# Moving fillers and small steps in the RWKV/attention stage of a fused decoder layer

## What is computed

```python
def layer_forward(x, c, attn_cache, rw_prev, rw_wkv, t5_table, lw):
    mod = (jax.nn.silu(c) @ lw['w_mod'] + lw['b_mod'])[:, None, :]
    sh1, sc1, gt1, sh2, sc2, gt2 = jnp.split(mod, 6, axis=-1)
    h = rms_norm(x, lw['norm1'], NORM_EPS) * (1.0 + sc1) + sh1
    q, k, v, p_rw, g_a, g_b = jnp.split(h @ lw['w_in'], IN_SPLITS, axis=-1)
    ...
    o_a = swa(q, k, v, ...)          # window of 128 keys, 8 query heads, 2 KV heads
    o_b, new_wkv = rwkv7_mix(p_rw, ...)
    m = jax.nn.sigmoid(g_a) * (o_a @ lw['w_pa']) + jax.nn.sigmoid(g_b) * (o_b @ lw['w_pb'])
    x = x + gt1 * (m @ lw['w_o'])
    h2 = rms_norm(x, lw['norm2'], NORM_EPS) * (1.0 + sc2) + sh2
    return x + gt2 * moe_ffn(h2, *lw['moe']), ...

def rwkv7_step(S, inp):              # one token; the kernel does the prompt in chunks of 64
    r_t, w_t, k_t, v_t, kk_t, a_t = inp
    sa = jnp.einsum('bhvk,bhk->bhv', S, -kk_t)
    S = (S * w_t[:, :, None, :] + sa[..., None] * (kk_t * a_t)[:, :, None, :]
         + v_t[..., None] * k_t[:, :, None, :])
    return S, jnp.einsum('bhvk,bhk->bhv', S, r_t)
```

## Time and profile before

| | |
|---|---|
| median of 3 runs | 1316.26 us (1314.79 to 1317.28) |
| the profiled execution, its own time | 1316.26 us |
| its span in the trace | 1314.5 us (1.8 us lie around it) |
| mean granted clock of PE | 0.99 |
| PE busy | 1254.3 us (95%) |
| DVE busy | 452.8 us (34%) |
| ACT busy | 300.0 us (23%) |
| POOL busy | 52.3 us (4%) |
| moved by DMA | 467 MB, 355 GB/s over the span |

### The profile page before, as it was taken

The page is one execution under the profiler, slowest core; times in us unless marked ns, Lnnn a source line. Parts: engine busy times, 40 slices in busy tenths (PEclk is TensorE's granted clock), DMA queues, the critical chain, the costliest instruction groups (busy, mean ns, idle before and its releaser), DMA issues.

```text
span 1314.5 us, 21012 instructions
## 1 busy us (share of the span) xinstructions
PE 1254.3 (95%) x8339; PEld 621.5 (47%) x8339; DVE 452.8 (34%) x1035; ACT 300.0 (23%) x554; POOL 52.3 (4%) x66
## 2 busy tenths in 40 slices
PE   6999997999989999999999999999999999999997
PEld 5887776987733333333333333333333333333333
DVE  2055648436342332222332222332222223322225
ACT  3013441210122222212221211221211122212112
POOL 0000621200000000000000000000000000000000
PEclk9999999999979999999999999999999999999999
DMA  9976251148459999999999999999999999999993
GB/s 365 358 255 248 100 164 67 36 179 342 193 202 406 426 428 428 428 430 429 426 430 429 428 428 429 428 428 430 426 428 430 429 427 429 429 428 428 430 428 164
DMA packets 55606, 467.05 MB, mean 355 GB/s; under 512 B 5141, under 2 KB 7449, under 8 KB 29690
## 3 DMA queue, kind: packets, MB, share of 16 engines
q1 hardware_dynamic: 53354, 461.07, 84.4%
q0 software_dynamic: 1664, 5.20, 1.4%
q10 hardware_dynamic: 544, 0.13, 0.0%
HBM read 463.91 MB, written 5.09 MB: 357 GB/s over the span
## 4 chain that ended last, share of the span: by engine, by line
PE 72%; DMA 20%; DVE 5%; ACT 2%; issue 1%; SPq 0%; DVEq 0%
PE ps L1346 25%; DMA ring<-in_w 18%; PE ps L1373 13%; PE ps L1294 6%; PE ps L865 5%; PE ps L1319 4%; PE ps L855 2%; DMA ring<-in_w_in 2%; PE ps L1253 2%; PE ps L1354 2%; PE ps L1221 1%; PE ps L1301 1%; PE ps L834 1%; ACT PT L751 1%; PE ps L874 1%
## 5 line engine op out<-in xcount | busy, mean ns | idle before, releaser
L1346 PE MATMUL ps<-ring,PT 128*64 128x512 f32 x1536 | 338.9, 595 | 8.0 <-DMA ring<-in_w 7.7
L1809 DVE TENSOR_TENSOR SQ<-ps,SQ 128x528 f32<-128x528 f32 x128 | 81.6, 699 | 611.1 <-PE ps L1319 611.1
L1346 PEld LDWEIGHTS ps<-ring,PT 128*64 128x64 f32 x1536 | 109.7, 137 | 231.1 <-issue 211.9
L1373 PE MATMUL ps<-ring,PT 128*64 128x512 f32 x768 | 170.1, 595 | 0.0
L746 ACT COPY HT<-ps 128x512 f32<-128x512 f32 x64 | 34.4, 589 | 394.0 <-PE ps L1346 394.0
L1346 PE MATMUL ps<-arena,PT 128*64 128x512 f32 x512 | 113.2, 593 | 2.6 <-DMA arena<-in_w 2.6
L1294 PE MATMUL ps<-XR,PT 128*64 128x512 f32 (+1 forms) x396 | 99.7, 622 | 1.1 <-DVE PT L1773 1.1
L1373 PEld LDWEIGHTS ps<-ring,PT 128*64 128x64 f32 x768 | 53.0, 137 | 100.0 <-issue 100.0
L1319 PE MATMUL ps<-PT 64*128 64x264 f32 x512 | 74.0, 408 | 0.0
L1346 PEld LDWEIGHTS ps<-arena,PT 128*64 128x64 f32 x512 | 36.5, 137 | 76.6 <-issue 70.6
L865 PE MATMUL ps<-HT,ring 128*128 128x264 f32 x304 | 69.4, 388 | 0.0
(11 more groups left out here) (424 smaller groups left out, 1152.4 us busy)
## 6 DMA issues: line engine op xcount, KB each, us to landing
ring<-in_w SPq DMA_DIRECT2D x144, 2048.0 KB, 27.1
arena<-in_w SPq DMA_DIRECT2D x48, 2048.0 KB, 27.7
ring<-in_w_mod SPq DMA_DIRECT2D x12, 2048.0 KB, 13.8
ring<-in_w_in SPq DMA_DIRECT2D x9, 2048.0 KB, 14.7
ring<-in_w_o SPq DMA_DIRECT2D x2, 2048.0 KB, 16.1
ring<-in_w_pa SPq DMA_DIRECT2D x1, 2048.0 KB, 12.8
ring<-in_w_pb SPq DMA_DIRECT2D x1, 2048.0 KB, 8.7
bias_rows<-bias_by_distance POOLq DMA_DIRECT2D x1, 1536.0 KB, 14.1
```

The lines of the kernel that those rows point to most:

```text
L1346: last = mm(ps[64 * lin:64 * lin + 64, 2 + hh, :], XG[:, k % 4, k // 4, :], slot_tile(slot, c)[:, k % 2, lin * FE + hh * 512:lin * FE + hh ...
L1373: last = mm(ps[64 * hh:64 * hh + 64, 4, :], AC[:, f, :], slot_tile(slot, c)[:, f % 4, hh * 512:hh * 512 + 512], start=(f == 0), stop=(f == ...
L1809: v.tensor_tensor(YA[:, p::4, :], ps[:, bank:bank + 2, 0:T], YA[:, p::4, :], ALU.add).then_inc(sem["comb_used"], 1)
```

## The change

It moves work within each engine's list; no arithmetic is added or removed apart from one reduction that is done whole and not in two halves.

1. Start of attention. PE does `gates(8)` right after the row transposes (L914) and ahead of the decay and rate matmuls; the transposes and the duplication of K and V come after the modulation transpose (L840), in PSUM banks 0 to 3, and PE waits for `qk_ready` there. `gates(12)` follows them and comes ahead of the wait for `kvrow_evac`. ACT does its `gates(0)` ahead of the decay evacuations, and the five K/V copies after `mod_columns(8)`, ahead of the exponentials. The `gates(4)` between the two first score groups is gone, and `gates(16)` becomes `gates(20)`.
2. Sample step on DVE. `sa` is reduced in one instruction, and this and the first state product come ahead of the two copies that raise `smp_att` to 2.
3. `SOE` and `BON` move on DVE from the third level of the inverse (i = 2) to right after the reduction `so`, ahead of the masks NR and KR.
4. `project([8])`: part 1 moves from ahead of the wait for `ot_ready` to behind L1188, and part 2 from there to behind the group norm's first sums, together with part 3.

```diff
--- before.py
+++ after.py
@@ -579,22 +579,22 @@
             act.wait_ge(sem["mixed"], 1)
             act.activation(XMv[:, 13, :], XMv[:, 13, :], ACT.Sigmoid).then_inc(sem["lora_in"], 1)
             act.activation(XMv[0:64, 12, :], XMv[0:64, 12, :], ACT.Tanh).then_inc(sem["lora_in"], 1)
+            gates(0)
             for hp in range(4):
                 act.activation(LD[:, hp, :], group(), ACT.Sigmoid, bias=par("rw_w0", hp)).then_inc(sem["a_evac"], 1)
             for hp in range(4):
                 act.activation(Aa[:, hp, :], group(), ACT.Sigmoid, bias=par("rw_a0", hp)).then_inc(sem["a_evac"], 1)
-            act.wait_ge(sem["kvrow_done"], 1)
-            act.copy(vr[:, 0:2, :], ps[:, 5, 0:2 * P].rearrange("p (a b) -> p a b", b=P))
-            act.copy(vr[0:NS, 2, :], ps[0:NS, 5, 2 * P:3 * P])
-            act.wait_ge(sem["kvrow_done"], 3)
-            act.copy(kd, ps[:, 6:8, 0:T])
-            act.copy(kvr[:, 0, :], ps[:, 6, T:T + P])
-            act.copy(kvr[0:NS, 1, :], ps[0:NS, 7, T:T + P]).then_inc(sem["kvrow_evac"], 1)
-            gates(0)
             act.wait_ge(sem["sh_t"], 4)
             for hp in range(4):
                 act.copy(GG[:, hp, :], group()).then_inc(sem["a_evac"], 1)
             mod_columns(8)
+            act.wait_ge(sem["kvrow_done"], 2)
+            act.copy(kd, ps[:, 0:2, 0:T])
+            act.wait_ge(sem["kvrow_done"], 3)
+            act.copy(vr[:, 0:2, :], ps[:, 2, 0:2 * P].rearrange("p (a b) -> p a b", b=P))
+            act.copy(vr[0:NS, 2, :], ps[0:NS, 2, 2 * P:3 * P])
+            act.copy(kvr[:, 0, :], ps[:, 3, 0:P])
+            act.copy(kvr[0:NS, 1, :], ps[0:NS, 3, P:2 * P]).then_inc(sem["kvrow_evac"], 1)
 
             act.wait_ge(sem["cs_ready"], 1)
             act.activation(eP, CS, ACT.Exp).then_inc(sem["decays"], 1)
@@ -687,11 +687,11 @@
                     wps[64 * s:64 * s + 64, :, :]).then_inc(sem["st_w"], 16)
 
 
-            project([8], range(1, 3))
+            project([8], range(1, 2))
             for hp in range(4):
                 act.wait_ge(sem["gn_done"], hp + 1)
                 act.mul(TMn[:, hp, :], ps[:, 4 + hp, 0:T], 1.0 / CH).then_inc(sem["gn_evac"], 1)
-            project([8], range(3, 4))
+            project([8], range(2, 4))
             mod_rows(10)
             mod_columns(10)
             bank = group()
@@ -914,29 +914,32 @@
                     last = tr(ps[0:9, 6 + i % 2, (c % 4) * P:(c % 4) * P + P], PTv[:, CR + c, NP - 1:T], ID)
                 last.then_inc(sem["sh_t"], 1)
 
-            pe.wait_ge(sem["qk_ready"], 1)
-            for n, (t0, nt) in enumerate(TILES):
-                last = tr(ps[0:nt, 5, n * P:n * P + P], PTv[:, CV, t0:t0 + nt], ID)
-            last.then_inc(sem["kvrow_done"], 1)
-            for kv, (t0, nt) in enumerate(TILES[1:]):
-                pe.wait_ge(sem["sh_evac"], 3 + kv)
-                mm(ps[:, 6 + kv, 0:T], II[64 * kv:64 * kv + 64, :], PTv[64 * kv:64 * kv + 64, CK, :], start=True, stop=True)
-                tr(ps[0:nt, 6 + kv, T:T + P], PTv[:, CK, t0:t0 + nt], ID).then_inc(sem["kvrow_done"], 1)
-
+            gates(8)
             pe.wait_ge(sem["ld_lw"], 64)
             pe.wait_ge(sem["lora_in"], 2)
             for hp in range(4):
                 mm(group()[:, 0:T], LWw[0:64, hp * P:hp * P + P], XMv[0:64, 12, :], start=True, stop=True).then_inc(sem["a_done"], 1)
             for hp in range(4):
                 mm(group()[:, 0:T], LWw[64:128, hp * P:hp * P + P], XMv[64:128, 12, :], start=True, stop=True).then_inc(sem["a_done"], 1)
-            gates(8)
             for hp in range(4):
                 mm(group()[:, 0:T], LWg[:, hp * P:hp * P + P], XMv[:, 13, :], start=True, stop=True).then_inc(sem["a_done"], 1)
             modulation_transposed(8)
+            pe.wait_ge(sem["sh_evac"], 4)
+
 
             pe.wait_ge(sem["a_evac"], a_end("modT8"))
+            pe.wait_ge(sem["qk_ready"], 1)
+            for kv in range(HKV):
+                mm(ps[:, kv, 0:T], II[64 * kv:64 * kv + 64, :], PTv[64 * kv:64 * kv + 64, CK, :],
+                   start=True, stop=True).then_inc(sem["kvrow_done"], 1)
+            for n, (t0, nt) in enumerate(TILES):
+                tr(ps[0:nt, 2, n * P:n * P + P], PTv[:, CV, t0:t0 + nt], ID)
+            for n, (t0, nt) in enumerate(TILES[1:]):
+                last = tr(ps[0:nt, 3, n * P:n * P + P], PTv[:, CK, t0:t0 + nt], ID)
+            last.then_inc(sem["kvrow_done"], 1)
+
+            gates(12)
             pe.wait_ge(sem["kvrow_evac"], 1)
-            gates(12)
             for h in range(HQ):
                 s = h % 2
                 last = mm(ps[:, 2 + s, NS * (h // 2):NS * (h // 2) + NS], II[64 * s:64 * s + 64, :], PTv[64 * s:64 * s + 64, h // 2, NP:T],
@@ -980,10 +983,9 @@
                 last.then_inc(sem["att_o"], 1)
 
             scores(0)
-            gates(4)
             pe.wait_ge(sem["qs_evac"], 1)
             scores(1)
-            gates(16)
+            gates(20)
             probabilities(0)
             scores(2)
             values(0)
@@ -1180,17 +1182,16 @@
                 last = mm(ps[64 * s:64 * s + 64, 2, hp * CH:hp * CH + CH], G4[64 * s:64 * s + 64, NCHUNK - 1, hp, :],
                           II[64 * s:64 * s + 64, 0:CH], start=True, stop=True)
             last.then_inc(sem["wps_done"], 1)
-            project([8], range(1, 2))
             pe.wait_ge(sem["carry_evac"], 5)
             pe.wait_ge(sem["ot_ready"], 1)
 
             pe.wait_ge(sem["soe_ready"], 1)
             mm(ps[:, 5, 0:32], SOE, cst[:, K_SL:K_SL + 32], start=True, stop=True).then_inc(sem["smp_o"], 1)
-            project([8], range(2, 3))
+            project([8], range(1, 2))
             pe.wait_ge(sem["smp_step"], 2)
             for hp in range(4):
                 mm(ps[:, 4 + hp, 0:T], BO, OT[:, hp, :], start=True, stop=True).then_inc(sem["gn_done"], 1)
-            project([8], range(3, 4))
+            project([8], range(2, 4))
             modulation(10)
             modulation_transposed(10)
             pe.wait_ge(sem["ld_r"], 32)
@@ -1582,12 +1583,11 @@
             chain(v.reciprocal(sm, sm))
             chain(v.tensor_scalar(Sx[:, 0:KEYS], Sx[:, 0:KEYS], sm, None, ALU.mult))
             done(v.tensor_scalar(Sx[:, P + NS:P + 2 * NS], cst[0:64, K_BB:K_BB + NS], Sx[:, P:P + 1], None, ALU.mult), "smp_att", 1)
-            chain(v.tensor_reduce(sa[:, 0:16], T1[:, 0:16, :], AX.X, ALU.add))
+            chain(v.tensor_reduce(sa, T1, AX.X, ALU.add))
+            chain(v.tensor_tensor(S0, S0, over_values(1), ALU.mult))
             dve.wait_ge(sem["smp_done"], 2)
             chain(v.tensor_copy(pTs, ps[:, 5, 0:64]))
             done(v.tensor_copy(PSf, ps[0:NS, 5, 64:128]), "smp_att", 2)
-            chain(v.tensor_reduce(sa[:, 16:32], T1[:, 16:32, :], AX.X, ALU.add))
-            chain(v.tensor_tensor(S0, S0, over_values(1), ALU.mult))
             dve.wait_ge(sem["smp_part"], 1)
             chain(v.tensor_tensor(S0, S0, T2, ALU.add))
             chain(v.tensor_tensor(T1, over_keys(sa), over_values(2), ALU.mult))
@@ -1607,6 +1607,10 @@
 
 
             chain(v.tensor_reduce(so, T1, AX.X, ALU.add))
+            done(v.tensor_tensor(SOE.rearrange("p (g v) -> p g v", v=32), so.unsqueeze(1).broadcast_to([P, 4, 32]),
+                                 cst[:, K_HM:K_HM + 4].unsqueeze(2).broadcast_to([P, 4, 32]), ALU.mult), "soe_ready", 1)
+            dve.wait_ge(sem["bon_evac"], 4)
+            chain(v.tensor_tensor(BON, BON, vv, ALU.mult))
             M2 = cst[:, K_M2:K_M2 + P].unsqueeze(1).broadcast_to([P, 8, P])
             for n in range(2):
                 for q, (M, name) in enumerate(((NR, "nr_ready"), (KR, "kr_ready"))):
@@ -1628,11 +1632,6 @@
                 dve.wait_ge(sem["y_done"], n + 1)
                 done(v.tensor_tensor(X[:, hs, :], bank(4 * n), Ib, ALU.add), "x_ready", n + 1)
             for i in range(1, len(LEVELS)):
-                if i == 2:
-                    done(v.tensor_tensor(SOE.rearrange("p (g v) -> p g v", v=32), so.unsqueeze(1).broadcast_to([P, 4, 32]),
-                                         cst[:, K_HM:K_HM + 4].unsqueeze(2).broadcast_to([P, 4, 32]), ALU.mult), "soe_ready", 1)
-                    dve.wait_ge(sem["bon_evac"], 4)
-                    chain(v.tensor_tensor(BON, BON, vv, ALU.mult))
                 for n in range(2):
                     hs = slice(8 * n, 8 * n + 8)
                     dve.wait_ge(sem["dx_done"], 2 * (i - 1) + n + 1)
```

## The result

The changed kernel takes 1323.76 us (median of 6 runs, 1321.17 to 1327.31), the kernel before 1316.74 (6 runs, 1309.55 to 1319.45). The ratio is 1.0058, with a 95% interval of 1.0039 to 1.0078: slower by 0.6%, some 7 us. The forecast was 1320.7, so the direction held and the loss was larger than forecast, just inside the upper end of the range. The profiled execution took 1323.0 us, with a span of 1321.2: 6.7 us more than before. All ratios here are worked out from the fast runs (one of the kernel before beside e1 to e4, 1464.22 us at a granted clock of 0.84, is not among them) and differ by up to 0.13% from the quotient of the two medians.

A forecast was written before the change was run, and what follows sets the result against it. The prediction read the chain as 72% PE and 20% DMA, the DMA share all in the expert loop. Terms 0.5 - 0.2 + 1.6 + 2.5 = +4.4 us on 1316.26 gave 1320.7 us, range 1317.5 to 1324.0.

The forecast's parts named there:

- The expert loop passes it on: Ahead of the expert loop, a microsecond gained or lost is one at the end, one to one.
- Part 1, PE and the weights: Attention start: gates(8) waits for weight chunk 5 until 127.7, decay ends at 135.5, gates(12) starts at 141.5.
- Part 1, DVE: Softmax at the attention start: POOL products hold DVE's small steps, probabilities ready at 159.4, +0.5 us.
- the rival without a fall: Clock stays full at the attention start's gates: -1.4 us there, sum +2.5, 1318.8 us; chance 0.14.
- Part 2: Sample reductions on DVE: merging gains, smp_att 2's 3.5 us lateness is hidden by 4.2 us of slack; -0.2 us.
- Part 3: SOE and BON ahead of NR and KR on DVE: no idle time in front to hide them, +1.6 us.
- Part 4: Last projection columns: PE stands idle ahead of ot_ready and this goes through to the end, +2.5 us.
- The clock falls once more, or for longer: Waits at about 199 and 277.5 bring one more half-clock stretch, costing 1.7 us: 1322.4 us; chance 0.22.

The follow-up runs named there:

- e1: Kernel before with only the attention start reordered (gates(8) ahead of the lora, K and V behind it): 1314.80 us, ratio 0.9999.
- e4: Kernel before with only the projection columns moved, none ahead of ot_ready: 1319.43 us, ratio 1.0045.
- e7: Kernel before with the attention start reordered and seven additional matmuls in PE's wait ahead of gates(8): 1312.72 us, ratio 0.9991.
- e10: The whole changed kernel with additional matmuls in its three PE waits (7 ahead of gates(8), 6 of smp_att 2, 5 of ot_ready): 1319.89 us, ratio 1.0045.
- e2: Kernel before with only the whole sample reduction and S0 product put ahead of the copies that raise smp_att 2: 1316.92 us, ratio 1.0017.
- e3: Kernel before with only SOE and BON moved ahead of NR and KR: 1315.71 us, ratio 1.0009.
- e11: Kernel before with nine additional matmuls in the router's idle time and one ahead of the lora: 1307.45 us, ratio 0.9951.
- e5: Kernel before with the projection columns moved and five additional matmuls in PE's wait ahead of ot_ready: 1316.44 us, ratio 1.0028.
- e9: Kernel before with the two sample reductions merged, but behind the copies that raise smp_att 2, S0 product unmoved: 1315.65 us, ratio 1.0004.
- e12: Kernel before with nine additional router matmuls and K and V first, two additional matmuls, gates(8), then the lora: 1311.14 us, ratio 0.9975.

## Why the forecast was right in direction and short in size

- **The expert loop passes it on.** Held: 6.80 us at the first load, 6.7 in the span.
- **Part 1, PE and the weights.** Held to 0.8 us: the gates waited until 128.08 (forecast 127.7), ran at half clock for 3.4 us, decay came at 136.19 (135.5), `gates(12)` at 140.68 (141.5).
- **Part 1, DVE.** The size failed, +0.5 forecast and -1.0 measured. The step was that L1555 is held by L446, L1557 by L453 and L1563 by L455. DVE was ready at 149.32, not 150.2, and L446 began at 149.86: the first three steps passed in 0.7 us and only L1562 and L1564 were held. DVE reached these steps 0.4 us later than before (forecast 1.4), and from them to the start of L1564 it took 5.7 us (forecast 6.5, before 7.4). The same step fails in the rival without a fall, -1.4 by the forecast: e7 and e10 have -3.3 and -2.8. In the trace of before L1555 started at 148.83, 0.10 behind L453; in e2's, with the old order, at 149.02, with L453 at 149.14, and that stage is 2.2 us shorter. The order of DVE and GpSimd is decided there by some tenths of a microsecond, so a forecast could only give both cases, each with its full price.
- **Part 2.** This is the step that failed most, forecast at -0.2 us and measured at +2.7: "the slack is 4.2 us, so the 3.5 are hidden with 0.7 to spare". The slack was read from a trace that happened to have full clock from 135 to 367 us. Four of the eight other traces with the old part 2 (e1, e3, e4, e11) have 3.4 or 6.8 us at half clock there, and the slack is 1.7 us in e1's and e11's, 2.9 in e3's and 3.2 in e4's, not 4.2. And the wait that the change adds lies just ahead of small work, with 10.2 us at half clock behind it in both unfilled traces: PE is 3.0 us late and then 3.8 to 4.1 us slower. The cost is +2.7 and +3.0; filled in e10 +0.2, with the copies first +0.3.
- **Part 3.** Held: +1.6 and +1.7, nothing given back later, and no idle time of DVE in front (L1610 and L1613 at 216.53 and 216.86).
- **Part 4.** The idle time held: 2.53 us, forecast 2.5. What was missing, put at nothing in the term, is the 1.6 to 1.7 us of clock behind it, shown by e5: the part cost +4.1 and +4.3.
- **The rival.** "The clock falls once more, or for longer" was the case that came, at 0.22. It had the mechanism and both places right, but the price of one stretch. The argument against it, PE's 3.6 us of idle time ahead of 212.56 without a fall, was one execution's. Two new stretches came, not one, and their price is not one figure: 1.6 to 1.7 us on the path in part 4, 3.8 us less slack in part 2.

By terms: forecast 0.5 - 0.2 + 1.6 + 2.5 = 4.4; the trace has -1.0 + 2.7 + 1.6 + 4.1, less 0.8 that the trace of before has lost by itself from 222 to 277 us, and 0.1 in the router: 6.7. That the forecast is off by only 2.3 us is in part luck: parts 2 and 4 were 4.5 us too low together, and part 1, 1.5 too high, and the 0.8 of the trace of before made up for half of it.

## What to carry to other kernels

Where an edit makes TensorE wait on the path, price the wait and then the work behind it at half clock; if something must stay in order there, give TensorE harmless full-size matmuls for the time of the wait, and look for such waits that were there all along (here 0.3% in the router). A slack read from one trace is one execution's: where it is a fraction of a microsecond, or rests on a full clock, take it as gone. And what a step raises for others goes ahead of what it computes for itself, even if merging looks cheaper.

## What the runs showed of the hardware

- The granted clock differs between executions of the same code: at 129 us six traces with the old start have 6.8 us at half clock and two have none, which are 4.8 us shorter in this stage than five of the six and 2.6 than the sixth (e2). The 31 executions of the kernel before beside e9 to e12 took 1309.12 to 1321.76 us at mean granted clocks of 0.983 to 0.992, and the two go together (correlation -0.69, some 1.15 us for each 0.001 of clock); that it is the fall at 129 that spreads them isn't shown.
- Matmuls whose result nobody uses can make a kernel faster: nine of them in the router give 4.7 us in the trace (3 to 4 against most others) and 0.34% in the times.
- GpSimd's L445 (four instructions from 145.70 to 149.77) did not hold DVE's L1556, which has two inputs in SBUF and took 0.16 us at 149.32, while products such as L453 hold such a step to their end (2.10 us for 4 elements at 152.64). The Trainium skill (SBUF — State Buffer, section "SBUF: two separate sides") gives the port pair to whichever starts first, for the whole instruction, by which L1556 should have been held until 149.77 and taken 0.6 us; here the measurement decides. The first such step passes beside L445 in e1, e3, e4, e7 and e10 too, in 0.16 to 0.26 us. In e2 a step with one input, L1556 of that kernel, was held for 2.29 us:

```profile
149.02 0.16 DVE L1555 TENSOR_TENSOR st<-st,sinkb 128x4 f32<-128x4 f32 x1
149.22 2.29 DVE L1556 TENSOR_SCALAR st<-st 128x4 f32<-128x4 f32 x1
151.55 0.16 DVE L1557 TENSOR_TENSOR st<-sinkb,st 128x4 f32<-128x4 f32 x1
```
